# Loading x by feature pairs from ScalarE's queue, and starting the first slab chunk by chunk

## The reference, cut to what matters

```python
def rms_norm(x, g):
    y = x * lax.rsqrt(jnp.mean(x * x, axis=-1, keepdims=True) + EPS)
    return y * g

def short_conv_mixer(h, w_in, conv_w, w_out):
    b_gate, c_gate, v = jnp.split(h @ w_in, 3, axis=-1)      # h: 512x1024, w_in: 1024x3072
    u = causal_depthwise_conv(c_gate * v, conv_w)            # width 3
    return (b_gate * u) @ w_out

# layer 0: x += short_conv_mixer(rms_norm(x, a_norm)); x += squared_relu_mlp(rms_norm(x, mlp_norm))
# shared keys and values; layer 1: x += diff_attention(...); x += squared_relu_mlp(...)
```

## Time and profile before

| what | value |
|---|---|
| runs | 1165.45, 1165.77 and 1167.9 us, median 1165.77 |
| span of the profiled execution | 1164.3 us |
| TensorE busy | 1148.2 us, 99% |
| VectorE busy | 634.3 us, 54% |
| ScalarE busy | 382.6 us, 33% |
| DMA from memory | 102.93 MB read, 90 GB/s over the span |
| instructions | 14392 |

### The profile page before, as it was taken

One profiled execution on the slowest core, in us unless ns is written; L12 is line 12 of the kernel. 1 busy time (PEld: TensorE's weight loads), 2 busy tenths in 40 slices (PEclk: granted clock), 3 DMA queues, 4 the chain that ended last, 5 costly groups with the idle time before them and its releaser, 6 DMA issues.

```text
span 1164.3 us, 14392 instructions
## 1 busy us (share of the span) xinstructions
PE 1148.2 (99%) x5432; PEld 948.5 (81%) x5432; DVE 634.3 (54%) x873; ACT 382.6 (33%) x586; POOL 119.0 (10%) x94
## 2 busy tenths in 40 slices
PE   7999999999999999999999999999999999999998
PEld 5888888888888888888888788788888888888887
DVE  5656555643543543555553799946643544544542
ACT  6212233321221221234432677735322222222221
POOL 0000012000000000012210355524000000000000
PEclk8999999999999999999999999999999999999999
DMA  5433333233233233232322111113433233233232
GB/s 149 111 104 95 109 91 101 81 108 109 76 106 109 77 104 108 78 101 94 108 91 73 42 32 37 37 40 98 116 107 109 75 108 108 73 108 109 73 95 86
DMA packets 201557, 105.77 MB, mean 91 GB/s; under 512 B 12576, under 2 KB 196896, under 8 KB 201504
## 3 DMA queue, kind: packets, MB, share of 16 engines
q1 hardware_dynamic: 200464, 105.03, 31.6%
q10 hardware_dynamic: 1040, 0.00, 0.0%
HBM read 102.93 MB, written 2.10 MB: 90 GB/s over the span
## 4 chain that ended last, share of the span: by engine, by line
PE 96%; DVE 2%; DMA 1%; ACT 1%; issue 1%; SPq 0%; ACTq 0%; DVEq 0%
PE ps L427 82%; PE ps L548 8%; PE ps L578 1%; PE ps L605 1%; PE ps L452 1%; DMA kv<-in_x 1%; PE ps L591 1%; PE ps L612 0%; PE ps L581 0%; PE ps L562 0%; DVE nmax L1190 0%; DVE work L1202 0%; PE ps L527 0%; DVE ah L1209 0%; PE ps L516 0%
## 5 line engine op out<-in xcount | busy, mean ns | idle before, releaser
L427 PE MATMUL ps<-h,w_hi 128*128 128x512 f32 x1792 | 557.5, 392 | 3.0 <-DVE h L978 2.6
L427 PEld LDWEIGHTS ps<-h,w_hi 128*128 128x128 f32 x1792 | 334.7, 189 | 71.3 <-issue 2.8
L427 PE MATMUL ps<-h,w_lo 128*128 128x512 f32 x896 | 349.8, 390 | 0.0
L427 PE MATMUL ps<-ah,w_hi 128*128 128x512 f32 x1024 | 315.9, 390 | 0.0
L738 ACT ACTIVATE w_hi<-w_raw 128x1024 fp32r<-128x1024 f32 x185 | 193.3, 1052 | 253.9 <-DMA w_raw<-in_w_up 110.7
L973 DVE TENSOR_TENSOR w_lo<-w_raw,w_hi 128x1024 fp32r<-128x1024 f32 x185 | 232.6, 1261 | 54.9 <-ACT w_hi L738 54.3
L427 PEld LDWEIGHTS ps<-ah,w_hi 128*128 128x128 f32 x1024 | 191.8, 188 | 39.7
L427 PE MATMUL ps<-ah,w_lo 128*128 128x512 f32 x512 | 199.3, 389 | 0.0
L427 PEld LDWEIGHTS ps<-h,w_lo 128*128 128x128 f32 x896 | 168.8, 188 | 35.7
L984 DVE TENSOR_TENSOR xT<-ps,xT 128x512 f32<-128x512 f32 x80 | 55.2, 690 | 205.4 <-PE ps L427 205.4
L796 ACT ACTIVATE ah<-work 128x512 fp32r<-128x512 f32 x64 | 40.5, 632 | 239.7 <-DVE work L1074 239.7
(11 more groups left out here) (105 smaller groups left out, 635.9 us busy)
## 6 DMA issues: line engine op xcount, KB each, us to landing
w_raw<-in_w_up SPq DMA_DIRECT2D x64, 512.0 KB, 4.0
w_raw<-in_w_down SPq DMA_DIRECT2D x64, 512.0 KB, 3.9
w_raw<-in_a_w_in SPq DMA_DIRECT2D x24, 512.0 KB, 3.7
w_raw<-in_w_kv SPq DMA_DIRECT2D x16, 512.0 KB, 3.5
w_raw<-in_a_w_out SPq DMA_DIRECT2D x8, 512.0 KB, 3.9
w_raw<-in_w_q SPq DMA_DIRECT2D x8, 512.0 KB, 4.0
w_raw<-in_w_o SPq DMA_DIRECT2D x8, 512.0 KB, 4.0
kv<-in_x SPq DMA_DIRECT2D x4, 512.0 KB, 6.0
```

What stands on the lines that cost most here:

```text
L427: last = nc.tensor.matmul(ps[:, bank, :], w[:, s, k * P:(k + 1) * P], src(half, k), start=(k == 0 and i == 0), stop=(k == KC - 1 and i == 2))
```

## The change

x is loaded by pairs of feature chunks (all 512 tokens of 256 features, rows of 1 KB), four transfers that ScalarE's queue issues behind the gains. SP starts with slab 0 in two halves of four chunks, with a semaphore of their own each, then slab 1 and slab 2, and only then the conv taps. TensorE transposes chunk by chunk, four tiles each, into the banks X_BANK, and makes the products of the first slab between the transposes, in the order: chunks 0 to 3 transposed, products 0 and 1, chunks 4 and 5 transposed, products 2 and 3, chunks 6 and 7 transposed (into banks 4 and 5 a second time, once their first contents are copied), products 4 to 7. The h pieces of the first norm are made straight from PSUM (x_hi on ScalarE, x_lo on VectorE). xT is filled by eight copies, all on ScalarE (x_copy): two behind the fourth h piece, six behind slab 1's split, and the squares come after them. Slab 0's split is made in two halves on both engines. TensorE waits before slab 2 for all eight copies, since slab 2 and slab 3 use banks 2 and 3.

```diff
@@ -48,6 +48,7 @@
 Q_BANK = (B_AT, B_Q)
 KV_BANKS = 6
 K_T_AFTER = 7
+X_BANK = (4, 5, 6, 7, 2, 3, 4, 5)
 WO_BANK = (B_Q, 1, 2, 3, 0, 1, 2, 3)
 WO_SPLITS = ((4, 5), (), (6,), (7,), (), (), (8,), (), (9,))
 
@@ -175,7 +176,10 @@
         h_of = [h1, h2, h1, h2, h1, h2, h1]
 
 
-        s_x = [sem(f"s_x{t}") for t in range(TB)]
+        s_x = [sem(f"s_x{c2}") for c2 in range(KC // 2)]
+        s_w0 = sem("s_w0")
+        s_w0hi = sem("s_w0hi")
+        s_w0lo = sem("s_w0lo")
         s_gain_a = sem("s_gain_a")
         s_conv = sem("s_conv")
         s_par = sem("s_par")
@@ -187,7 +191,6 @@
         s_zero = sem("s_zero")
         s_cst = sem("s_cst")
         s_xt = sem("s_xt")
-        s_xd = sem("s_xd")
         s_xa = sem("s_xa")
         s_hi = sem("s_hi")
         s_lo = sem("s_lo")
@@ -267,18 +270,16 @@
             def cols(w, c):
                 return w[:, :, c * P:(c + 1) * P]
 
-            def load_x(t):
-                sp.dma_start(x_tok[:, t, :], x_d[:, t, :]).then_inc(s_x[t], 16)
-
-            for t in range(TB - 1):
-                load_x(t)
+            sp.dma_start(w_raw[:, 0, 0:4 * P].rearrange("p (k c) -> p k c", k=4),
+                         win_d[:, 0:4, KC * P:(KC + 1) * P]).then_inc(s_w0, 16)
+            sp.dma_start(w_raw[:, 0, 4 * P:8 * P].rearrange("p (k c) -> p k c", k=4),
+                         win_d[:, 4:8, KC * P:(KC + 1) * P]).then_inc(s_raw[0], 16)
 
             for j in range(KC):
                 for i, part in enumerate((1, 2, 0)):
-                    load(S_IN + 3 * j + i, cols(win_d, part * KC + j))
-                    if j == 0 and i == 0:
-                        load_x(TB - 1)
-                    if j == 0 and i == 1:
+                    if j or i:
+                        load(S_IN + 3 * j + i, cols(win_d, part * KC + j))
+                    if j == 0 and i == 2:
                         with nc.allow_non_contiguous_dma(reason="conv taps: one float a feature"):
                             sp.dma_start(conv[:, :, :], a_conv.rearrange("l w (k p) -> p (l w) k", p=P)).then_inc(s_conv, 16)
                 if j == 2:
@@ -457,20 +458,43 @@
                 spread(BC, lambda t: rcol[:, i, t:t + 1].to_broadcast([P, P]), s_nbc)
 
 
+            def transpose_x(c):
+
+                pe.wait_ge(s_x[c // 2], 16)
+                if c >= 6:
+                    pe.wait_ge(s_xa, c - 5)
+                    pe.wait_ge(s_lo, c - 5)
+                for t in range(TB):
+                    last = nc.tensor.transpose(ps[:, X_BANK[c], t * P:(t + 1) * P], x_tok[:, t, c * P:(c + 1) * P], ident[:])
+                last.then_inc(s_xt, 1)
+
+            def first_slab(k):
+                if k == 0:
+                    pe.wait_ge(s_w0lo, 1)
+                if k == 4:
+                    wait_slab(S_IN)
+                return product(0, S_IN, operand(I_A), (k,), chunks_of(I_A))
+
             pe.wait_ge(s_zero, 5)
             pe.wait_ge(s_cst, 5)
-            for t in range(TB):
-                pe.wait_ge(s_x[t], 16)
-                for hf in range(2):
-                    for k in range(4):
-                        c = (4 * hf + k) * P
-                        last = nc.tensor.transpose(ps[:, 2 * t + hf, k * P:(k + 1) * P], x_tok[:, t, c:c + P], ident[:])
-                    last.then_inc(s_xt, 1)
-            pe.wait_ge(s_xd, TB - 1)
-            pe.wait_ge(s_xa, TB + 1)
-
-            for n in range(N_IN):
-                dense(S_IN + n, U_IN + n, I_A, n == 0)
+            for c in range(4):
+                transpose_x(c)
+            for k in range(2):
+                first_slab(k)
+            for c in range(4, 6):
+                transpose_x(c)
+            for k in range(2, 4):
+                first_slab(k)
+            for c in range(6, KC):
+                transpose_x(c)
+            for k in range(4, KC):
+                last = first_slab(k)
+            last.then_inc(s_used, 1)
+
+            for n in range(1, N_IN):
+                if n == 2:
+                    pe.wait_ge(s_xa, KC)
+                dense(S_IN + n, U_IN + n, I_A)
                 if n == 1:
                     norm_sums(NORM_A)
                 if n == 2:
@@ -729,6 +753,9 @@
         def _(act):
             with nc.allow_non_contiguous_dma(reason="gains: one float a feature"):
                 act.dma_start(gains[:, g_a, :], a_norm.rearrange("l (k p) -> p (l k)", p=P)).then_inc(s_gain_a, 16)
+            for c2 in range(KC // 2):
+                two = slice(c2 * 2 * P, (c2 + 1) * 2 * P)
+                act.dma_start(x_tok[:, :, two], x_d[:, :, two]).then_inc(s_x[c2], 16)
 
             def split(n, off=0):
 
@@ -750,22 +777,32 @@
                 act.wait_ge(s_nbc, count)
                 nc.scalar.activation(rB[:], ps[:, BC, :], ACT.Copy).then_inc(s_rB, 1)
 
-            for t in range(TB):
-                if t == TB - 1:
-                    split(0)
-                    act.wait_ge(s_xt, 2 * t + 1)
-                    nc.scalar.activation(xT[:, 0:4, t * P:(t + 1) * P],
-                                         ps[:, 2 * t, :].rearrange("p (k q) -> p k q", k=4), ACT.Copy).then_inc(s_xa, 1)
-                act.wait_ge(s_xt, 2 * t + 2)
-                nc.scalar.activation(xT[:, 4:8, t * P:(t + 1) * P],
-                                     ps[:, 2 * t + 1, :].rearrange("p (k q) -> p k q", k=4), ACT.Copy).then_inc(s_xa, 1)
+            def x_hi(c):
+
+                act.wait_ge(s_xt, c + 1)
+                nc.scalar.activation(h1[:, 0, c, :], ps[:, X_BANK[c], :], ACT.Copy, scale=gains[:, g_a, c:c + 1]).then_inc(s_hi, 1)
+
+            def x_copy(c):
+                act.wait_ge(s_lo, c + 1)
+                nc.scalar.activation(xT[:, c, :], ps[:, X_BANK[c], :], ACT.Copy).then_inc(s_xa, 1)
+
             act.wait_ge(s_gain_a, 16)
-            act.wait_ge(s_xd, TB - 1)
-            act.wait_ge(s_xa, TB + 1)
-            for m in range(KC):
-                chunk_hi(I_A, m, g_a)
-                if m == 5:
-                    split(1)
+            x_hi(0)
+            act.wait_ge(s_w0, 16)
+            nc.scalar.activation(w_hi[:, 0, 0:4 * P], w_raw[:, 0, 0:4 * P], ACT.Copy).then_inc(s_w0hi, 1)
+            x_hi(1)
+            x_hi(2)
+            act.wait_ge(s_raw[0], 16)
+            nc.scalar.activation(w_hi[:, 0, 4 * P:8 * P], w_raw[:, 0, 4 * P:8 * P], ACT.Copy).then_inc(s_whi, 1)
+            x_hi(3)
+            x_copy(0)
+            x_copy(1)
+            for c in range(4, KC):
+                x_hi(c)
+            split(1)
+            for c in (4, 5, 2, 3, 6, 7):
+                x_copy(c)
+            act.wait_ge(s_xa, KC)
             for m in range(KC):
                 square(NORM_A, m)
             for n in range(N_IN):
@@ -998,18 +1035,24 @@
             mixed[0] += 1
             dve.wait_ge(s_zero, 3)
             V.tensor_copy(identb[:], ident[:]).then_inc(s_cst, 1)
-            for t in range(TB - 1):
-                dve.wait_ge(s_xt, 2 * t + 1)
-                V.tensor_copy(xT[:, 0:4, t * P:(t + 1) * P],
-                              ps[:, 2 * t, :].rearrange("p (k q) -> p k q", k=4)).then_inc(s_xd, 1)
-            split(0)
+            def x_lo(c):
+                dve.wait_ge(s_hi, c + 1)
+                V.scalar_tensor_tensor(h1[:, 1, c, :], ps[:, X_BANK[c], :], gains[:, g_a, c:c + 1],
+                                       h1[:, 0, c, :].bitcast(F32), ALU.mult, ALU.subtract).then_inc(s_lo, 1)
+
             dve.wait_ge(s_gain_a, 16)
-            dve.wait_ge(s_xd, TB - 1)
-            dve.wait_ge(s_xa, TB + 1)
-            for m in range(KC):
-                chunk_lo(I_A, m, g_a)
-                if m == 5:
-                    split(1)
+            x_lo(0)
+            dve.wait_ge(s_w0hi, 1)
+            V.tensor_tensor(w_lo[:, 0, 0:4 * P], w_raw[:, 0, 0:4 * P], w_hi[:, 0, 0:4 * P].bitcast(F32),
+                            ALU.subtract).then_inc(s_w0lo, 1)
+            x_lo(1)
+            x_lo(2)
+            dve.wait_ge(s_whi, 1)
+            V.tensor_tensor(w_lo[:, 0, 4 * P:8 * P], w_raw[:, 0, 4 * P:8 * P], w_hi[:, 0, 4 * P:8 * P].bitcast(F32),
+                            ALU.subtract).then_inc(s_wlo, 1)
+            for c in range(3, KC):
+                x_lo(c)
+            split(1)
 
             for m in range(KC):
                 dve.wait_ge(s_sq, m + 1)
```

## The result

The changed kernel takes 1169.88 us (median of 6 runs, 1168.68 to 1171.02), the kernel before, run beside it, 1166.19. The ratio is 1.0029, with a 95% interval of 1.0019 to 1.0039: slower by 0.3%, 3.4 us. The spans of the two profiled executions differ by 3.1 us (1167.4 against 1164.3).

The account below looks back on a forecast made before the run. TensorE, busy for 99% of the span, was taken to bound the kernel. Slab 2 starting 0.3 us earlier and a fallen clock costing 2.4 sum to +2.1 on 1165.8: 1167.9 us, range 1164.4 to 1170.4.

Parts of the forecast that it names:

- ScalarE's row plus a fallen clock: Start of slab 2: ScalarE's copies and squares set it and the clock falls; 1166.0 to 1169.8 us, chance 0.62.
- its two terms: At slab 2: when it starts, -0.3 us against 29.01, and what clock it gets, +2.4 us.
- Issue: At the start: reordered load issue costs nothing; table load ends before 5 us, ScalarE's first work comes after 7.
- Landing of x: Start of the kernel: pair 0 lands at 6.7 us, pairs 1 to 3 near 9.0, 10.7 and 12.0.
- TensorE up to chunk 7: Transposes and early products: chunk 7 transposed at 16.2 us, ends 14.6 and 18.0.
- The slow case of the forecast: TensorE up to chunk 7: early products at 1.28 us each put chunk 7 at 16.8 us.
- From chunk 7 to slab 2: ScalarE's h piece, split, six copies, squares and slab 2's split take 12.5 us; slab 2 starts at 28.7.
- The pause: TensorE after slab 1: idle 2.5 us for the sums of squares, then 0.7 us before slab 2.
- The clock: In or just behind the pause TensorE's clock falls, costing slab 2 2.4 us, ends 0 and 4.7.
- Rival 1: In the new pause before slab 2 the clock holds: -0.3 us, 1165.5; chance 0.18.
- Rival 2: ACT queue: x comes late, chunk 7 near 18.5, slab 2 at 31.0; +4.4 us, 1170.2; chance 0.13.
- Rival 3: Slab 2 follows slab 1 without a hole, so slab 1's 3.5 us gain stays: 1162.3; chance 0.07.

Follow-up runs that it names:

- e6_table: The changed kernel plus a one-column activation ahead of ScalarE's first wait, to make the table load early; 1170.03 us, ratio 1.0027 to the kernel before.
- e5_spx: The changed kernel with the four x loads back on SyncE's queue, pair 0 ahead of all; 1168.69 us, ratio 1.0022 to the kernel before.
- e10_act: The combined kernel e8_all, but with x loaded from ScalarE's queue behind the gains, weights from SyncE; 1164.05 us, ratio 0.9978 to the kernel before.
- e8_all: The changed kernel with the edits of e5_spx, e6_table, e3_plain and e7_late5 together; 1162.39 us, ratio 0.9965 to the kernel before.
- e9_warm: e8_all plus twelve idle identity products on TensorE, seven before pair 0 and five before pair 1; 1161.38 us, ratio 0.9956 to the kernel before.
- e2_defer: The changed kernel with three of ScalarE's six x copies moved behind slab 2's split; 1167.22 us, ratio 1.0006 to the kernel before.
- e4_late: The changed kernel with slab 2 split before squares and sums, norm sums behind slab 2, scales spread in mid slab 3; 1167.59 us, ratio 1.0008.
- e7_late5: e4_late plus slab 5's split moved ahead of the wait for rB on both engines; 1165.09 us, ratio 0.9988 to the kernel before.
- e1_fill: The changed kernel plus eleven unread matmuls on TensorE behind slab 1, before the norm sums; 1168.46 us, ratio 1.0016 to the kernel before.
- e3_plain: The changed kernel with all eight chunks transposed before slab 0's products; loads, queues and splits unchanged; 1165.78 us, ratio 0.9995 to the kernel before.

## Why the prediction was right, and where it was off

The forecast was +2.1 us, just inside what counts as no change; measured were +3.4 by the ratio and +3.1 in the trace. The case that had most of the chance (ScalarE's row plus a fallen clock) is the one that came, with both signs of it in the trace; the time is in the range, and in that case's own range by the spans' difference (the median, 1169.88, is 0.1 above it). What should have been called likelier is "slower". That the sum is off by 1.0 only is in part luck, since its two terms were off by more and in opposite ways: slab 2 was to start 0.3 us earlier than before and started 1.5 later (30.51, at the very end of the interval of 27.1 to 30.5), and the clock was to cost 2.4 and cost 1.6 in the profiled execution. Nearly all of the first error is the time of chunk 7.

- **Issue.** Right in effect. Behind the first wait, the taps cost SP 0.58 us instead of 3.40, and no wait comes of them. The table load was put at before 5 us; it came at 8.45, behind the wait for the first transposes, and so delayed ScalarE's first work by 1.28 us. e6_table shows that it was hidden nevertheless, by the wait for pair 1 and not by the cover I had named.
- **Landing of x.** This is a term that was mis-sized: pair 0 at 6.7 was 7.28, pair 1 at 9.0 was 10.23. I had given the first 4.5 us the old rate; the rows of after show nothing up to 1.5 and then 132 and 126 GB/s, 0.39 MB by 4.5, where the sum needed more than 0.52 MB. With the missing 0.13 MB added to the 0.79 at 355 GB/s, the sum gives 7.1. e5_spx shows that queue and order matter, since with pair 0 in front it landed at 4.87; whether the gains ahead of it or the weights beside it held it back is not separated. The Trainium skill, "DMA: Bandwidth & Descriptors", section "Issuing engines are not separate DMA queues", says that loads started by several engines share the same DMA engines and save only the time of issuing them. The traces agree in this sense: ScalarE's queue brought x no sooner than SyncE's did (pair 0 at 8.08 in e10_act, at 4.85 in e8_all).
- **TensorE up to chunk 7.** 16.2 was taken, 17.8 came, the upper half of the interval. 1.2 of it is pair 1, the rest the pace: the first two products took the slow pace in part (2.52 us, 11.96 to 14.48, against 1.9 in the mean that was taken). The slow case of the forecast, 16.8, was the better one. The Trainium skill, "TensorE: Matmul & The Clock Gate", section "What's actually happening", has the lower clock as the state at rest, released by activity. The traces agree: with 16.8 and the late pair 1 the sum gives 18.0, and with idle products ahead of them the transposes of e9_warm take 0.14 us instead of 0.23. The recorded 1.00 at the start is not the pace that the work has.
- **From chunk 7 to slab 2.** 12.5 forecast, 12.7 measured (17.8 to 30.51). The six copies were put at 3.15 with their wait and took 3.07 (19.49 to 22.56). e2_defer shows the copies' share, e4_late and e7_late5 that without the squares ahead of it slab 2 is ready in time. This was called the step that decided, and its size was right to 0.2 us.
- **The pause.** 2.5 and 0.7 us forecast, 2.31 and 0.52 measured, with the releasers named.
- **The clock.** It fell as forecast, and cost 1.6 instead of 2.4, two and a half chunks' worth of slow pace instead of four. That is the cost in one execution. In the trace of e6_table, which differs only in the table load, slab 2 takes 7.92 us to the spread, 2.3 more than before, so the forecast's 2.4 is not refuted. e1_fill gave back 1.6 between slab 2 and the spread and 1.4 by the medians, with nothing else moved.
- **Rival 1** (the clock holds) fell in this kernel. With a pause of 0.8 us (e2_defer) or 0.95 (e3_plain) instead of 2.31 the clock did hold. **Rival 2** came in part: chunk 7 later than 16.5, and each us beyond it lost. **Rival 3** fell; its gain appears only when slab 2 no longer waits for the squares.

## What to carry to other kernels

A start that is made earlier is worth what the next wait lets through: follow the moved work to the first point from which the bounding engine no longer stops, and write down, engine by engine, what stands in order ahead of the thing it waits for there. Here six copies and eight squares stood ahead of a split that only needed its raw weights. Moving that split and slab 5's ahead was worth 4.8 us (e7_late5), while landing pair 0 2.4 us sooner was worth 1.2 by the medians (e5_spx). A pause on TensorE like the one of 2.3 us here should be priced twice, once as itself and once as the slow clock behind it (1.6 and 2.3 us in two traces); and filling a wait with early products is no gain when they stand ahead of what another engine is waiting for.

## What the runs showed of the hardware that was not expected

- Work whose result nobody reads made kernels faster twice: 2.65 us of it in a pause (e1_fill, 1.4 us by the medians), and 4.6 us of it while x was on its way (e9_warm, the last three groups of eight transposes 1.09 to 1.11 us each, where e8_all took 5.46 for the three).
- The granted clock reads 1.00 from the start of every trace here, also where the work has the pace of the lower level. In e5_spx the second product takes 1.28 us (11.61 to 12.89) at a recorded 1.00, as much as a product in slab 0 of the kernel before at 0.50 (16.30 to 17.58), and not the 0.68 of slab 1. At the start of a trace the distance between the starts says more than the column.
- ScalarE's table load was made behind the wait of the first activation in the change (8.45), where in the kernel before it stood ahead of that wait (1.24). An activation of one column put ahead moved it to 4.32. Why the change moved it was not tried.
- The attention heads (some 636 to 763 us of the span) take 124.4 or 124.5 us in the profiled executions of the kernel before, the change, e1_fill, e3_plain, e8_all and e9_warm, and 125.3 to 125.5 in those of e2_defer, e4_late, e5_spx, e6_table, e7_late5 and e10_act. It comes with no difference in the code of that stage. The traces show the granted clock: near 740 us TensorE waits 1.1 us for VectorE in each of the twelve, and the twelve matmuls behind that wait take 1.66 or 1.67 us in the first group, at clock 1.00. In the second group the clock is at its lower level there for some 3 us, and they take 2.30 to 2.90. The change and e10_act, a row of the timeline and the stretch of it:

```profile
745.22 1.67 PE L629 MATMUL ps<-ah 128*128 128x256 f32 x12 [1.13 <-DVE ah L1252]
745.20:746.90 1.70, 1.68 (x13) 1.56 (x13) 1.63 (x5) 0.19 (x1) 1.01 (x2) 1.00 0.00 0
...
739.71 2.90 PE L627 MATMUL ps<-ah 128*128 128x256 f32 x12 [1.13 <-DVE ah L1256]
739.70:742.60 2.90, 2.89 (x13) 2.75 (x13) 2.76 (x7) 0.19 (x1) 2.20 (x2) 0.50 0.00 0
```

So the same wait takes the clock in some executions and not in others; what decides it stays open.
